# Adding the gathered rows of the second expert table tile by tile, with TensorE's four column groups on four feature chunks

## What is computed

```python
def peer(xn, w_query, sub_keys_1, sub_keys_2, expert_u, expert_v):
    # ... per token and head (8 heads): the 16 best of 128*128 experts, with softmax gates
    def token_block(args):
        xb, idx, g = args
        u = jnp.take(expert_u, idx, axis=0)
        a = jnp.einsum('thkd,td->thk', u, xb)
        hid = jax.nn.gelu(a) * g
        vsel = jnp.take(expert_v, idx, axis=0)
        return jnp.einsum('thk,thkd->td', hid, vsel)
```

## Time and profile before

| | us |
|---|---|
| median of 3 runs | 3038.62 |
| lowest, highest | 3035.63, 3040.16 |
| span of the profiled execution | 3036.7 |
| TensorE busy in it | 2648.2 (87%) |
| VectorE, ScalarE, GpSimd busy | 1834.3, 1177.7, 862.2 |
| TensorE idle before the adds (L2246), waiting for tiles | 310.0 |

### The profile page before, as it was taken

One profiled execution on the slowest core, in us unless ns is written; L12 is line 12 of the kernel. 1 busy time (PEld: TensorE's weight loads), 2 busy tenths in 40 slices (PEclk: granted clock), 3 DMA queues, 4 the chain that ended last, 5 costly groups with the idle time before them and its releaser, 6 DMA issues.

```text
span 3036.7 us, 42765 instructions
## 1 busy us (share of the span) xinstructions
PE 2648.2 (87%) x16156; PEld 2092.0 (69%) x16156; DVE 1834.3 (60%) x2504; ACT 1177.7 (39%) x2290; POOL 862.2 (28%) x568
## 2 busy tenths in 40 slices
PE   8999899999999988999999999978865577777773
PEld 7886699999999988989999898656532322222220
DVE  6888555455555555464445468878677764455555
ACT  1003443333333344435334444655455532222233
POOL 0000000000000000040000003645568887676776
PEclk9999999999999999999999999999976678888887
DMA  6342545555555553443555657999999999999998
GB/s 241 139 149 104 204 159 188 181 192 180 189 183 189 183 180 129 154 152 140 188 185 194 235 206 271 407 416 403 402 359 384 379 394 410 410 413 418 422 410 350
DMA packets 128588, 796.62 MB, mean 262 GB/s; under 512 B 30546, under 2 KB 30546, under 8 KB 31762
## 3 DMA queue, kind: packets, MB, share of 16 engines
q0 software_dynamic: 75712, 417.94, 34.4%
q1 hardware_dynamic: 52736, 376.90, 33.6%
HBM read 923.45 MB, written 4.19 MB: 305 GB/s over the span
## 4 chain that ended last, share of the span: by engine, by line
PE 53%; DMA 16%; DVE 13%; issue 9%; POOL 6%; ACT 2%; DVEq 1%; POOLq 0%; SPq 0%; ACTq 0%
PE bank L1806 14%; PE bank L1808 14%; PE bank L1807 14%; DMA s_u<-in_expert_u,s_u_index 9%; DMA s_v<-in_expert_v,s_v_index 7%; PE bank L1894 4%; DVE s_u L1683 4%; POOL s_u L581 3%; POOL s_v L599 3%; PE bank L2246 3%; DVE s_cacc L1215 2%; DVE s_w_lo L1126 1%; DVE s_yrow L1369 1%; ACT s_w_hi L626 1%; PE bank L1936 1%
## 5 line engine op out<-in xcount | busy, mean ns | idle before, releaser
L1126 DVE TENSOR_TENSOR s_w_lo<-s_raw,s_w_hi 128x2048 fp32r<-128x2048 f32 x258 | 592.5, 2296 | 655.1 <-ACT s_w_hi L626 654.7
L626 ACT ACTIVATE s_w_hi<-s_raw 128x2048 fp32r<-128x2048 f32 x256 | 489.9, 1914 | 656.7 <-PE bank L1808 656.7
L1806 PE MATMUL bank<-s_a_hi,s_w_hi 128*128 128x256 f32 x2560 | 720.9, 282 | 5.5 <-DVE s_w_lo L1126 3.6
L1807 PE MATMUL bank<-s_a_lo,s_w_hi 128*128 128x256 f32 x2560 | 721.3, 282 | 0.0
L1808 PE MATMUL bank<-s_a_hi,s_w_lo 128*128 128x256 f32 x2560 | 720.5, 281 | 0.0
L2246 PE MATMUL bank<-s_v,s_spread 128*32 128x512 f32 x2048 | 322.7, 787 | 312.7 <-DMA s_v<-in_expert_v,s_v_index 310.0
L1806 PEld LDWEIGHTS bank<-s_a_hi,s_w_hi 128*128 128x128 f32 x2560 | 484.4, 189 | 12.5 <-DVE s_w_lo L1126 5.9
L1808 PEld LDWEIGHTS bank<-s_a_hi,s_w_lo 128*128 128x128 f32 x2560 | 485.4, 190 | 0.0
L599 POOL DMA_INDIRECT s_v<-in_expert_v,s_v_index x256 | 428.8, 1675 | 189.5 <-PE bank L2246 95.0
L1807 PEld LDWEIGHTS bank<-s_a_lo,s_w_hi 128*128 128x128 f32 x2560 | 481.4, 188 | 0.5
L1683 DVE CUSTOM_DVE_ANT_0 s_u<-s_u,s_xn_late 128x2048 f32<-128x2048 f32 x128 | 293.6, 2294 | 271.2 <-DMA s_u<-in_expert_u,s_u_index 262.4
(11 more groups left out here) (316 smaller groups left out, 3057.0 us busy)
## 6 DMA issues: line engine op xcount, KB each, us to landing
s_raw<-in_stream SPq DMA_DIRECT2D x292, 1024.0 KB, 4.8
s_raw<-in_expert_v SPq DMA_DIRECT2D x32, 1024.0 KB
s_raw<-in_dense_u SPq DMA_DIRECT2D x29, 1024.0 KB
s_u<-in_expert_u,s_u_index POOLq DMA_INDIRECT x256
s_v<-in_expert_v,s_v_index POOLq DMA_INDIRECT x256
...
```

What stands on the lines that cost most here:

```text
L626: act.activation(w_hi[s % 2][:, :], raw[s][:, :], ACT.Copy).then_inc(hi_ready, 1)
L1126: dve.tensor_tensor(w_lo[s % 2][:, :], raw[s][:, :], w_hi[s % 2][:, :].bitcast(f32), ALU.subtract)\
L1806: pe.matmul(dst, left[0], right[0], start=start, stop=False)
L1807: pe.matmul(dst, left[0], right[1], start=False, stop=False)
```

## The change

**Slots and adds.** `adds` now takes one tile (k) instead of a group. It waits for the spread at the group's first tile and for its own tile alone. Its four matmuls have the same weights, the 128x32 block of quarter q, and take the four feature chunks of the tile into the four column groups of one bank. `v_used` rises once per tile, so gather_v(k) waits for tile k - 8 instead of for the group that holds it. The layout of the sums in PSUM is turned with it: bank 4t + q now holds token quarter q, and its partitions 32c to 32c + 31 hold feature chunk c.

**What follows from the layout.** `residual` and `dense_v_panel` write the same banks, so each of their matmuls with 128 weight columns becomes four with 32. `result` copies a token quarter of all features, and SP stores it with four DMAs of 32x512.

**Order.** A turn's second panel (of either table) stands between the adds of the group's second and third tile, where it stood behind all adds. A third one (turns 0 and 1 alone) stays behind them.

The diff, cut to its core:

```diff
@@ sync @@
             for t in range(TT):
-                for c in range(4):
-                    sp.wait_ge(out_ready, 4 * t + c + 1)
-                    part = slice(c * 512, (c + 1) * 512)
-                    sp.dma_start(out[t * 128:(t + 1) * 128, part], out_row[:, t, part]).then_inc(stored, 16)
-            sp.wait_ge(stored, 16 * 4 * TT)
+                for q in range(4):
+                    sp.wait_ge(out_ready, 4 * t + q + 1)
+                    for c in range(4):
+                        sp.dma_start(out[t * 128 + q * Q:t * 128 + (q + 1) * Q, c * 512:(c + 1) * 512],
+                                     out_row[c * Q:(c + 1) * Q, t, q * 512:(q + 1) * 512]).then_inc(stored, 16)
+            sp.wait_ge(stored, 16 * 16 * TT)
@@ gpsimd, gather_v @@
-                wait(pool, v_used, (k - NV) // 4 + 1)
+                wait(pool, v_used, k - NV + 1)
@@ scalar, spreads @@
-                wait(act, v_used, g + 1 - NW)
+                wait(act, v_used, 4 * (g + 1 - NW))
@@ tensor, residual @@
-                for c in range(4):
-                    part = slice(c * 512, (c + 1) * 512)
-                    ins = pe.matmul(bank[4 * t + c][:, :], ident[:, :], xres_late[:, part] if t else xres[:, 0, part], start=True, stop=False)
+                for q in range(4):
+                    for c in range(4):
+                        part = slice(c * 512, (c + 1) * 512)
+                        ins = pe.matmul(bank[4 * t + q][c * Q:(c + 1) * Q, :], ident[:, q * Q:(q + 1) * Q],
+                                        xres_late[:, part] if t else xres[:, 0, part], start=True, stop=False)
@@ tensor, dense_v_panel @@
-                    for c in range(4):
-                        ins = pe.matmul(bank[4 * t + c][:, :], ha[:, d, t * 128:(t + 1) * 128], raw[r][:, c * 512:(c + 1) * 512],
-                                        start=False, stop=d == DENSE - 1 and t == 0)
+                    for q in range(4):
+                        for c in range(4):
+                            ins = pe.matmul(bank[4 * t + q][c * Q:(c + 1) * Q, :], ha[:, d, t * 128 + q * Q:t * 128 + (q + 1) * Q],
+                                            raw[r][:, c * 512:(c + 1) * 512], start=False, stop=d == DENSE - 1 and t == 0)
@@ tensor, adds @@
-            def adds(g):
-
+            def adds(k):
+
+                g, q = divmod(k, 4)
                 t, last = g // (PH * GROUPS), g == ROUTES * GROUPS - 1
-                pe.wait_ge(spread_ready, g + 1)
-                for q in range(4):
-                    k = 4 * g + q
-                    pe.wait_ge(v_loaded[k % NV], (k // NV + 1) * 16)
+                if q == 0:
+                    pe.wait_ge(spread_ready, g + 1)
+                pe.wait_ge(v_loaded[k % NV], (k // NV + 1) * 16)
                 for c in range(4):
-                    for q in range(4):
-                        ins = pe.matmul(bank[4 * t + c][q * Q:(q + 1) * Q, :], spread[g % NW][:, q, :],
-                                        v_slot[(4 * g + q) % NV][:, c * 512:(c + 1) * 512], start=False, stop=last)
-                    if last:
-                        ins.then_inc(acc_done, 1)
-                if not last:
+                    ins = pe.matmul(bank[4 * t + q][c * Q:(c + 1) * Q, :], spread[g % NW][:, q, :],
+                                    v_slot[k % NV][:, c * 512:(c + 1) * 512], start=False, stop=last)
+                if last:
+                    ins.then_inc(acc_done, 1)
+                else:
                     ins.then_inc(v_used, 1)
@@ tensor, the loop over turns @@
-                if i >= 1:
-                    adds(i - 1)
-                for d in u_panels_in(i)[1:]:
+                for q in range(4):
+                    if i >= 1:
+                        adds(4 * (i - 1) + q)
+                    if q == 1:
+                        for d in u_panels_in(i)[1:2]:
+                            dense_u_panel(d)
+                        for d in v_panels_in(i)[1:]:
+                            dense_v_panel(d)
+                for d in u_panels_in(i)[2:]:
                     dense_u_panel(d)
-                for d in v_panels_in(i)[1:]:
-                    dense_v_panel(d)
```

14 lines of the change are left out of this document (7 added, 7 removed).

## The result

| | before | after |
|---|---|---|
| median of 20 runs each on one chip, us | 3037.67 | 3043.62 |
| ratio of the two | | 1.0015, 95% interval 1.0009 to 1.0022 |
| span of the profiled execution, us | 3036.7 | 3046.8 |
| TensorE busy, us | 2648.2 | 2693.8 |

The change costs 0.15%, about 4.6 us. That is within the 0.2% that I called no change, on its slow side, and outside my range, whose upper end was 3037. Executions of one kernel differ by some 5 us either way, and the profiled one of after is a long one: it took 3048.9. So I use its rows for where and how, and for sizes the runs, or means over several kernels' profiles. One of the 20 runs of before took 7011.45 us; it does not move the median.

The account below looks back on a forecast made before the run. It took DMA transfers as the bound, their queue starved by GpSimd's waits. Terms -6 - 6 - 5 + 1 = -16 us gave 3020.7 from the span and 3022.6 from the median; it predicted 3023 us, 80% range 3004 to 3037.

Parts of the forecast that it names:

- no change: Whole kernel: time within 0.2%, 6 us, of before, because the queue hides the stalls or nothing releases earlier; chance 0.22.
- The waits of GpSimd vanish: Expert-table gather stage: GpSimd's waits for the adds' line fall from 95.0 us to under 15.
- I am wrong if the waits vanish and the rates stay: Gather stage: stated failure sign; rates were to rise to 415 GB/s or above (1900 to 2200) and 419 (2500 to 2960).
- Up to 2200, -6: Stretch 1900 to 2200, first table's gathers and panels: filling rate dips behind stalls saves 6 us of at most 10.6.
- 2200 to 2500, -6: Stretch of gathers alone: saves 6 us of at most 20, with GpSimd taken as full for 280 of 300.
- Second panels between tiles, "nothing": TensorE's order: panels after the second tile add nothing; if wait cover went, some 3 us each in 6 groups.
- 2500 to 2960, -5: Stretch of the second table's gathers and panels: saves 5 us, half of the 10.8 us bound.
- Panels in column groups: Second table's panels on TensorE: four column groups run beside each other, 7.28 us a panel, nothing for the sum.
- The tail, +1: Kernel's end: adds at the low clock and four stores in place of one cost between -0.1 and +2 us, taken as +1.
- About as much again between two at most: Tail stores: SP takes 0.33 us for one and at most about that between two, so 1.0 to 2.0 us more.
- the queue hides it: Rival for DMA stalls: queued transfers absorb them, 3034 to 3038 us; chance 0.22 together with no earlier release.
- slower by over 0.2%: Whole kernel: mostly small loss from a colder clock and stores without gain, some from column-group packing; chance 0.10.

Follow-up runs that it names:

- e1: The changed kernel, but GpSimd's gather of tile k waits again for the whole group of tile k - 8; 3043.52 us, ratio 1.0011 to before.
- e2: The changed kernel with all second panels behind the four tiles again; 3039.21 us, ratio 1.0000 to before.
- e15: The changed kernel with only the second table's panels between tiles, the first table's behind all four; 3040.42 us, ratio 1.0000 to before.
- e16: The changed kernel with only the first table's panels between tiles, the second table's behind all four; 3044.97 us, ratio 1.0017 to before.
- e3: The kernel before with the new layout alone (panels, copies, stores), adds and slot releases still by group; 3045.22 us, ratio 1.0017 to before.
- e10: The kernel before with each store split into four of 32x512, 32 in all; 3041.78 us, ratio 1.0016 to before.
- e13: The changed kernel with half of the second half's stores issued by ScalarE's queue; 3040.85 us, ratio 0.9999 to before.

## Why the prediction was wrong

**The waits of GpSimd vanish: right.** 95.0 us became 1.5. The step from there was the weak one. I wrote that such waiting "is worth what it takes from the rate" and then took a part of the rate's gap to a full queue as its worth in each stretch (6 of 10.6 us, 6 of 20 and 5 of 10.8). e1 keeps 42.7 us of these waits and takes the same time; after has them as dot waits. The condition that I set down, "I am wrong if the waits vanish and the rates stay", is nearly what happened.

**Up to 2200, -6: measured 0.** The rate rose by 5 GB/s, but tile 63 is reached at 2144.9 for 2144.5 (means). The dip of 374 at 2060 became 404, and no tiles were gained by it; that the extra bytes were panels and SP's next transfers, work brought forward, fits SP's rows but was not counted. My dips were real; filling them did not bring the tiles sooner. ("Last sixteen slices, from about 1898 us on" should have been fifteen; nothing hangs on it.)

**2200 to 2500, -6: measured +7.7** by the gathers' starts and +7.1 by the dots' (tiles 63 to 143), the largest miss. I had written that GpSimd is full for 280 of 300 us there, and still took a gain. Full means that the stretch is set by how long gathers take, and I held their length fixed. It is not. How the loss divides depends on the scale. By the gathers 4.2 us come with adding by tile, 3.2 of them from tile 95 to 143 (198.8 for 195.6), where half dots make before and after equal, and 3.5 with the panels between; by the dots it is 1.6 and 5.5. The dots also put most of it early: 5.0 of the 7.1 us stand between tiles 63 and 95 (156.9 for 151.9), where the rate dips behind 2220, and 2.1 from 95 to 143, where GpSimd is full.

**Second panels between tiles, "nothing": wrong.** I costed them on TensorE alone and named its waits as cover. That held. What I left out is what a panel's end releases: `panel_used`, and with it SP's transfers, 13.6 us sooner, which is the likely cause. By the runs the panels between cost 0.15% (e2 to after) and 0.17% (e15 to e16), and at tile 239 3.6 us by the gathers, 3.3 by the dots. The single traces of e15 and e16 do not show a gap at their ends; the means over three and four kernels do.

**2500 to 2960, -5: right in direction, half in size.** 414 to 419 GB/s, as forecast, and 2.8 us from tile 143 to 239 by the dots. The 7.1 us by the gathers are mostly GpSimd further ahead.

**Panels in column groups: right.** 7.03 to 7.7 us. The Trainium skill's 3.07x (TensorE: Matmul & The Clock Gate, Part 3) is measured there on four row tiles with K=32, and these are four column tiles with all 128 rows. For this form the trace shows more: 64 records of 0.446 us are 28.5, and took 7.03.

**The tail, +1: mis-sized, +2.7.** "About as much again between two at most" was a guess at a row that I did not have; a store is 0.46 us when SP has the next one ready, so 16 of them are 7.37 us and not hidden by four copies. (The range of 5.38 to 6.58 us for adds after idleness left out a row of 5.03; the last adds took 6.14.)

Put together, kernels with first-table panels between against those by group, by the dots: 0.4 us later at tile 63, 7.5 at 143, 4.8 at 239, 5.1 at the last dot and 5.5 at the last copy's end, and the stores make it 8.2. The runs give 4.6. The profiled executions of the four are 2.2 us over their kernels' medians in the mean, and those of before, e3 and e10 0.3 under, so about 2.5 of the 8.2 are chance. The remaining 5.7 and the 4.6 agree within what single executions can tell, and no closer. The rival that came nearest is "the queue hides it", with a price of its own on top. I gave slower by over 0.2% a chance of 0.10 and no change 0.22; the fault was to count dips that the stall could fill as time, to hold the length of a gather fixed, and to count no cost of a transfer that comes too soon.

**Open.** Why gathers start earlier in a dot, and so are held longer, when adds go by tile is not shown; only that by their gathers all eleven kernels which do so take longer from tile 95 to 143 (196.9 us and up) than the four by group (196.8 at most), and that short dots end it. By their dots the six with panels behind show no such loss there (199.6 us for 199.4). The three steps of 5 us rest on ratios with intervals of 0.1% either way. Some of the last stretch is unexplained: the last tile of the first table landed 18.5 us after its gather's start in after and 13.5 in before, but 13.7 in e13 and 16.1 in e10, with no pattern by kernel.
